# Second feed-forward matrix by seven products of quarters instead of eight

## The chip, the cores and the metric

The kernel runs on one core of one Trainium2 chip, as one program. The metric is the device time of one execution in microseconds (us); less is better. A core has five engines that run side by side, each through its own list of instructions in order, and that wait for one another by semaphores: TensorE (PE) for matrix products into PSUM, VectorE (DVE), ScalarE (ACT), GpSimd (POOL), and SyncE (SP), which here only issues transfers. PSUM has eight banks of 128 x 512 float32 numbers.

## What is computed

A network of two layers, for 1024 frames of a new stream and 8 x 16 frames of running ones (1152 frames of width 1024 together). Each layer is a mixer (attention and two kinds of recurrent memory) and a feed-forward part; the change lies in the feed-forward part alone:

```python
h = _rmsnorm(x, norm_ffn[layer])
x = x + jnp.square(jax.nn.relu(h @ w_ff1[layer])) @ w_ff2[layer]
```

`h` is 1152 x 1024, `w_ff1` 1024 x 4096, `w_ff2` 4096 x 1024.

## The kernel before

**Numbers in two parts.** Every large product runs on fp32r operands, which are the float32 numbers cut shorter. ACT copies a number into its fp32r high part, and a subtraction (`tensor_tensor` with `ALU.subtract`) makes the low part, the number less its high part. A product is then three matmuls, high x high, high x low and low x high (`PASSES`), added up in PSUM. Weights arrive by a transfer of 1 MB, a slab of 128 x 2048, in one of the two buffers of `raw`; ACT makes the high part (`hi_of`, L240), POOL the low part (`lo_of`, L245), both into one of the two buffers of `split`. The semaphores of this chain: `raw_in` (landed), `hi_ready`, `lo_ready`, `slab_begun` (PE has begun a slab, so the one before is free).

**Blocks.** The 4096 hidden features of a layer go in 8 blocks of 512 (`BLOCKS`), of which the first seven are a loop on each engine and the last is written out. A block takes four slabs: two of `w_ff1` (256 features each) and two of `w_ff2` (512 features x 512 outputs each).

- Hidden part (`proj_fm`, L452): for each of four groups of 128 features, 72 matmuls with 384 columns, 8 chunks of the width x 3 passes x 3 thirds of the frames, in three banks of PSUM (3, 4, 5 or 0, 1, 2 in turn). ACT takes the group out of PSUM with the relu (L624) into a row of 1152, DVE squares it (L651), ACT makes its high part (L614) and DVE its low part (L653). A low part reads two tensors in SBUF, as the square does.
- Second part (`pieces`, L571): 18 outputs of 128 frames x 512 features (9 tiles of frames, 2 halves), each 4 chunks x 3 passes = 12 matmuls of 512 columns: 216 in a block. DVE adds each finished bank to the stream `x` in SBUF (L658); this addition reads one tensor in SBUF and one in PSUM.

There are 16 such blocks in the program. The order of each engine is the order in which the code issues, and PE waits for `ff_lo` (low parts of the hidden rows), `lo_ready` (weights) and `ff_add` (a bank has been read). SP's loop `mlp` waits for `lo_ready` before it loads a slab in a buffer of `raw`.

## Time and profile before

| | |
|---|---|
| median of 3 runs | 3137.39 us (3136.26 to 3139.37) |
| the profiled execution, its own time | 3130.79 us |
| its span in the profile, mean granted clock | 3128.7 us, 0.978 |
| PE busy | 2967.5 us, 95% |
| matmuls of the hidden part and of projections like it (L452) | 7344, of which 288 in each block |
| matmuls of the second matrix (L571) | 3456 = 16 x 216 |

The profile is of one execution. Each engine's busy time is the time in which it ran instructions; a matmul's own duration overlaps that of the next, so its cost is read from the distance between starts, not from its mean. "PEclk" is the clock that TensorE was granted, 1.00 for 2.4 GHz and 0.50 for 1.2 GHz. The feed-forward parts lie at about 857 to 1657 us and 2330 to 3120 us of the span.

### The profile page before, as it was taken

To read this page: it belongs to the slowest core of one execution; us is meant where nothing else is said; L and a number is where in the kernel's file an instruction comes from. 1 tells how busy PE (TensorE), PEld (TensorE's weight loads), DVE (VectorE), ACT (ScalarE), POOL (GpSimd) and SP (SyncE) were. 2 spreads that over 40 slices of the span, in tenths; PEclk is the share of its full clock that TensorE was granted. 3 is DMA by queue.
4 is the path that set the end of the run, shared out by engine and by line. 5 is a ranking of instruction groups with operands and counts; after the bars stand their busy time and mean duration, and the time that the engine had idled before them with its cause. 6 is when DMAs were issued, how large, how long until landed. Compare 5 with 4: busy or idle time off the path is not lost.

```text
span 3128.7 us, 41812 instructions
## 1 busy us (share of the span) xinstructions
PE 2967.5 (95%) x17906; PEld 2751.8 (88%) x17906; DVE 1002.5 (32%) x1659; ACT 821.1 (26%) x1252; POOL 751.7 (24%) x476
## 2 busy tenths in 40 slices
PE   5999988888999999999999999897899999999998
PEld 5999977688999988999888999886898999899987
DVE  4500236564322222222232410295342222222223
ACT  4421346352312111121123302352231121111112
POOL 1122345132112111112112132473211112111111
PEclk8999999999999999999999999999999999999999
DMA  3112230233111111111103121203311111101111
GB/s 129 41 41 72 84 109 2 72 109 137 34 41 40 54 40 40 40 40 40 54 28 109 58 87 56 105 1 101 131 38 41 40 40 40 54 27 54 40 41 61
DMA packets 120320, 185.38 MB, mean 59 GB/s; under 512 B 11333, under 2 KB 84257, under 8 KB 119428
## 3 DMA queue, kind: packets, MB, share of 16 engines
q1 hardware_dynamic: 108784, 139.97, 13.6%
q0 software_dynamic: 11280, 43.50, 3.9%
q8 instruction: 94, 1.54, 0.2%
q14 instruction: 30, 0.25, 0.0%
q10 hardware_dynamic: 132, 0.13, 0.0%
HBM read 150.34 MB, written 33.20 MB: 59 GB/s over the span
## 4 chain that ended last, share of the span: by engine, by line
PE 87%; DVE 5%; ACT 2%; issue 2%; POOL 1%; DMA 1%; DVEq 0%; POOLq 0%; ACTq 0%; SPq 0%
PE ps L452 41%; PE ps L571 25%; PE ps L462 13%; PE ps L1383 1%; PE ps L1364 1%; DVE small L2259 1%; PE ps L401 1%; DMA units<-x_prompt 1%; PE ps L1689 1%; DVE units_r L527 0%; DVE spare L354 0%; PE ps L1729 0%; ACT spare L2128 0%; DVE spare L2520 0%; DMA units<-state_gla_s 0%
## 5 line engine op out<-in xcount | busy, mean ns | idle before, releaser
L452 PE MATMUL ps<-units_r,split 128*128 128x384 f32 x7344 | 1290.3, 336 | 10.8 <-DVEq L265 10.8
L452 PEld LDWEIGHTS ps<-units_r,split 128*128 128x128 f32 x7344 | 1283.6, 189 | 18.2 <-issue 18.1
L245 POOL TENSOR_TENSOR split<-raw,split 128x2048 fp32r<-128x2048 f32 x100 | 461.7, 4617 | 1728.2 <-ACT split L240 1728.2
L571 PE MATMUL ps<-split,units_r 128*128 128x512 f32 x3456 | 788.8, 389 | 0.4 <-DVE units L658 0.4
L571 PEld LDWEIGHTS ps<-split,units_r 128*128 128x128 f32 x3456 | 647.9, 188 | 134.8 <-issue 1.2
L462 PE MATMUL ps<-split,units_r 128*128 128x256 f32 x3456 | 425.1, 285 | 20.9 <-DVE units_r L527 19.3
L462 PEld LDWEIGHTS ps<-split,units_r 128*128 128x128 f32 x3456 | 420.0, 193 | 22.4 <-issue 19.4
L240 ACT ACTIVATE split<-raw 128x2048 fp32r<-128x2048 f32 x100 | 190.8, 1908 | 851.9 <-PE ps L571 433.6
L658 DVE TENSOR_TENSOR units<-units,ps 128x512 f32<-128x512 f32 x288 | 197.4, 687 | 496.7 <-PE ps L571 496.7
L651 DVE TENSOR_TENSOR spare<-spare 128x1152 f32<-128x1152 f32 x32 | 43.5, 1359 | 353.1 <-ACT spare L624 353.1
L651 DVE TENSOR_TENSOR glrow<-glrow 128x1152 f32<-128x1152 f32 x32 | 43.5, 1359 | 272.9 <-ACT glrow L624 272.9
L624 ACT ACTIVATE spare<-ps 128x1152 f32<-128x1152 f32 x32 | 36.2, 1132 | 281.4 <-PE ps L452 281.4
L624 ACT ACTIVATE glrow<-ps 128x1152 f32<-128x1152 f32 x32 | 36.2, 1132 | 280.2 <-PE ps L452 280.2
L521 DVE TENSOR_TENSOR units<-units,ps 128x256 f32<-128x256 f32 x72 | 30.3, 421 | 139.5 <-PE ps L462 135.8
L1670 PE MATMUL ps<-lend 128*128 128x128 f32 x480 | 61.0, 288 | 12.0 <-DVE lend L2509 8.9
L1670 PEld LDWEIGHTS ps<-lend 128*128 128x128 f32 x480 | 60.4, 205 | 13.4 <-issue 11.5
L1364 PE MATMUL ps<-masks,units 128*128 128x128 f32 x288 | 43.7, 279 | 19.1 <-DVE units L2269 11.3
L1896 ACT ACTIVATE units<-ps,small 128x128 f32<-128x128 f32 (+3 forms) x64 | 47.3, 739 | 42.8 <-DVE small L2259 42.7
L653 DVE TENSOR_TENSOR units_r<-glrow,units_r 128x1152 fp32r<-128x1152 f32 x32 | 43.5, 1358 | 39.5 <-ACT units_r L614 39.5
L653 DVE TENSOR_TENSOR units_r<-spare,units_r 128x1152 fp32r<-128x1152 f32 x32 | 43.5, 1358 | 39.5 <-ACT units_r L614 39.5
L2259 DVE TENSOR_REDUCE small<-ps 128x1 f32<-128x128 f32 (+3 forms) x64 | 48.4, 757 | 23.1 <-PE ps L1353 22.0
L324 ACT ACTIVATE glrow<-units 128x1024 f32<-128x1024 f32 x36 | 38.4, 1065 | 66.0 <-DVE units L658 44.1
(369 smaller groups left out, 2264.6 us busy)
## 6 DMA issues: line engine op xcount, KB each, us to landing
raw<-w_ff SPq DMA_DIRECT2D x64, 1024.0 KB, 5.4
raw<-w_in_even SPq DMA_DIRECT2D x14, 1024.0 KB, 5.2
raw<-w_in_odd SPq DMA_DIRECT2D x12, 1024.0 KB, 5.5
raw<-w_out SPq DMA_DIRECT2D x8, 1024.0 KB, 8.9
units<-x_prompt SPq DMA_DIRECT2D x4, 1536.0 KB, 9.2
stream<-units POOLq DMA_DIRECT2D x1, 4608.0 KB, 14.1
...
```

Source lines behind the costliest of these rows:

```text
L240: act.activation(split[:, n % 2, 0, :], raw[:, n % 2, :], ACT.Copy).then_inc(hi_ready, 1)
L245: pool.tensor_tensor(split[:, n % 2, 1, :], raw[:, n % 2, :], split[:, n % 2, 0, :], ALU.subtract).then_inc(lo_ready, 1)
L452: last = pe.matmul(ps[:, bank + n, 0:GN], weights(slab, a, k, c0, P), h[b][:, k, n * GN:(n + 1) * GN], start=(k == 0 and q == 0), stop=(k ...
L462: last = pe.matmul(out, h[b][:, k, n * P:(n + 1) * P], weights(slab, a, k, 0, COLS), start=(k == 0 and q == 0), stop=(k == KC - 1 and q == 2))
L571: one = pe.matmul(ps[:, bank, :], hid[b][:, k, n * P:(n + 1) * P], weights(base + 2 + half, a, k, 0, 512, 512), start=(k == 0 and q == 0), ...
L624: act.activation(as_groups(HTMP_[j % 2]), ps[:, b:b + 3, 0:GN], ACT.Relu).then_inc(ff_relu, 1)
L651: dve.tensor_tensor(tmp, tmp, tmp, ALU.mult).then_inc(ff_sq, 1)
L653: dve.tensor_tensor(hid[1][:, j], tmp, hid[0][:, j], ALU.subtract).then_inc(ff_lo, 1)
L658: dve.tensor_tensor(xx, xx, ps[:, bank, :], ALU.add).then_inc(ff_add, 1)
L1364: last = pe.transpose(ps[:, 4 + t // 4, (t % 4) * P:(t % 4 + 1) * P], PR[j % 4][:, t * P:(t + 1) * P], ident)
L1670: last = pe.matmul(out[:, h], EL[n % 2][:, l, h], EL[n % 2][:, l, h], start=True, stop=True)
L2259: dve.tensor_reduce(stat[:, 4 + j % 4:5 + j % 4], src, AX.X, ALU.min).then_inc(f_mx, 1)
```

## The change

In each of the seven looped blocks of a layer (14 blocks), the second part no longer multiplies the block of hidden values (1024 prompt frames x 512 features) by the block of weights (512 x 1024) in eight products of quarters. With the hidden values in quarters p11, p12 (frames 0 to 511, features 0 to 255 and 256 to 511), p21, p22 (frames 512 to 1023), and the weights in b11, b12, b21, b22, it makes seven products of sums and differences of quarters. The sums are made in place: of the hidden quarters by DVE (three instructions: p11 - p21, p21 + p22, and that less p11, and later a fourth, p12 less the result), of the weights' quarters by POOL (`minus`, four instructions). Each is then split in high and low part, by ACT and DVE on the left, by ACT and POOL on the right. The ninth tile (the 128 frames of the running streams) is computed from the plain quarters. Two running sums stay in PSUM: a product is added to a bank that already holds an earlier one, after that one has been read by an addition of DVE. The eighth block of each layer is as before.

The numbers of instructions in a looped block:

| | before | after |
|---|---|---|
| PE, matmuls of 512 columns | 216 | 192 |
| PE, matmuls of 384 columns | 288 | 288 |
| DVE, two tensors in SBUF | 8 of 1152 | 4 of 1152, 11 of 1024, 2 of 256 |
| DVE, additions out of PSUM | 18 | 31 |
| ACT | 4 relus, 4 high parts of 1152, 4 of 2048 | 4 relus, 7 + 8 high parts of 1024, 2 of 256, 2 of 2048 |
| POOL | 4 of 2048 | 2 of 2048, 12 of 1024 |

DVE's eleven instructions on quarters are four sums and seven low parts. The core of the diff; `slabs_done` counts the semaphores, which step 10 and 14 times a block now, and waits elsewhere in the kernel use it:

```diff
+        STEPS, SPLITS, READS = 10, 14, 31
+        BEGUN, HI, LO = STEPS - 4, STEPS - 4, SPLITS - 4
+        def slabs_done(n, more):
+            return n + 1 + (BLOCKS - 1) * more * sum(n >= base + 4 * (BLOCKS - 1) for base in (MLP0, MLP1))
...
+        X_BANK, Y_BANK = (6, 7, 0, 1), (2, 3, 4, 5)
+        SUMS_FIRST, SUMS_LAST = (0, 1, 2, 3), (2, 3, 0, 1)
...
+            return hidden_[:, 2 * c:2 * c + 2, 512 * r:512 * r + 512]
+        def right_slot(base, s, part):
+            return split[:, (base + s // 2) % 2, part, 1024 * (s % 2):1024 * (s % 2) + 1024]
...
                     if j >= 2:
                         pe.wait_ge(ff_relu, blk * HC + (layer * FF // P + j - 1))
-                    proj_fm(pe, hidden_bank(j), slab, (j % 2) * P, h).then_inc(ff_h, 1)
+                    proj_fm(pe, hidden_bank(j), base + j // 2, (j % 2) * P, h).then_inc(ff_h, 1)
+            def product(bank, left, slot, start, stop, first, more=False):
+                for k in range(2):
+                    for q, (a, b) in enumerate(PASSES):
+                        last = pe.matmul(ps[:, bank, :], left(b, k), right_slot(base, slot, a)[:, 512 * k:512 * k + 512],
+                                         start=(start and k == 0 and q == 0), stop=(stop and k == 1 and q == 2),
...
+            def summed_block(blk):
+                hidden_rows(blk, blk * SPLITS + splits)
+                def right(count):
+                    pe.wait_ge(lo_ready, blk * SPLITS + (splits + count))
+                def left(count):
+                    pe.wait_ge(ff_lo, blk * 9 + (lows + count))
+                def taken(count):
+                    pe.wait_ge(ff_add, blk * READS + (reads + count))
+                right(2)
+                left(1)
+                for n in SUMS_FIRST:
+                    if n == 2:
+                        pe.wait_ge(ff_relu, blk * HC + (layer * FF // P + HC))
+                    product(X_BANK[n], tile(a0, n), 0, True, True, n == 0).then_inc(ff_y, 1)
+                left(2)
+                product(5, ninth(0), 0, True, False, False)
+                right(4)
+                product(4, ninth(0), 1, True, True, True).then_inc(ff_y, 1)
+                right(7)
+                left(5)
+                product(5, ninth(1), 2, False, True, True).then_inc(ff_y, 1)
+                for n in SUMS_FIRST:
+                    if n >= 2:
+                        taken(3 + n)
+                    product(Y_BANK[n], tile(a1, n), 2, True, True, False).then_inc(ff_y, 1)
+                right(9)
+                for n in SUMS_FIRST:
+                    taken(7 + n)
+                    product(Y_BANK[n], tile(a2, n), 3, True, True, n == 0).then_inc(ff_y, 1)
+                right(10)
+                left(6)
+                for n in SUMS_FIRST:
+                    taken(1 + n)
+                    product(X_BANK[n], tile(a0, n), 0, False, True, n == 0, True).then_inc(ff_y, 1)
+                right(11)
+                left(7)
+                for n in SUMS_FIRST:
+                    taken(15 + n)
+                    product(X_BANK[n], tile(a1, n), 1, False, True, n == 0, True).then_inc(ff_y, 1)
+                right(12)
+                left(8)
+                for n in SUMS_FIRST:
+                    taken(11 + n)
+                    product(Y_BANK[n], tile(a2, n), 2, False, True, n == 0, True).then_inc(ff_y, 1)
+                right(13)
+                left(9)
+                taken(23)
+                product(2, ninth(1), 3, True, True, True).then_inc(ff_y, 1)
+                for n in SUMS_LAST:
+                    taken(19 + n)
+                    product(X_BANK[n], tile(a0, n), 3, False, True, False, True).then_inc(ff_y, 1)
+                taken(29)
...
+            def summed_block(blk):
+                def loaded(slab):
+                    act.wait_ge(raw_in[slab % 2], blk * 32 + raw_count(slab))
+                def freed(count):
+                    act.wait_ge(slab_begun, blk * STEPS + (begun + count))
+                def made(count):
+                    act.wait_ge(lo_ready, blk * SPLITS + (splits + count))
+                def squared(count):
+                    act.wait_ge(ff_sq, blk * 8 + (squares + count))
+                def relu(j):
+                    act.wait_ge(ff_h, blk * HC + (layer * FF // P + j + 1))
+                    b = hidden_bank(j)
+                    act.activation(as_groups(plain[:, j]), ps[:, b:b + 3, 0:GN], ACT.Relu).then_inc(ff_relu, 1)
+                def right_high(slot, src):
+                    act.activation(right_slot(base, slot, 0), src, ACT.Copy).then_inc(hi_ready, 1)
+                def left_high(slot, src):
+                    act.activation(slot, src, ACT.Copy).then_inc(ff_hi, 1)
+                loaded(base + 1)
+                freed(1)
+                act.activation(split[:, (base + 1) % 2, 0, :], raw[:, (base + 1) % 2, :], ACT.Copy).then_inc(hi_ready, 1)
+                relu(0)
+                relu(1)
+                loaded(base + 2)
+                freed(2)
+                right_high(0, right_raw(base, 0, 0))
+                squared(2)
+                left_high(a0[:, 0], quarter(plain, 0, 0))
+                left_high(left_ninth[:, 0, 0:2], plain[:, 0:2, SEQ:T])
+                loaded(base + 3)
+                right_high(1, right_raw(base, 0, 1))
+                squared(3)
+                left_high(a2[:, 0], left_third(layer))
+                relu(2)
+                relu(3)
+                freed(3)
+                right_high(2, right_raw(base, 1, 0))
+                squared(5)
+                left_high(a1[:, 0], quarter(plain, 0, 1))
+                left_high(left_ninth[:, 0, 2:4], plain[:, 2:4, SEQ:T])
+                made(5)
+                right_high(3, right_raw(base, 0, 1))
+                squared(7)
+                freed(4)
+                left_high(a0[:, 0], quarter(plain, 0, 0))
+                made(6)
+                right_high(0, right_sum)
+                freed(5)
+                right_high(1, right_raw(base, 0, 0))
+                freed(6)
+                left_high(a1[:, 0], quarter(plain, 1, 0))
+                made(8)
+                right_high(2, right_raw(base, 1, 0))
+                freed(7)
+                left_high(a2[:, 0], quarter(plain, 1, 1))
+                right_high(3, right_raw(base, 1, 1))
+                squared(8)
+                freed(8)
+                left_high(a0[:, 0], quarter(plain, 0, 1))
+                loaded(base + 4)
+                freed(9)
+                act.activation(split[:, base % 2, 0, :], raw[:, base % 2, :], ACT.Copy).then_inc(hi_ready, 1)
+                act.wait_ge(ff_lo, blk * 9 + (lows + 9))
...
+            def summed_block(blk):
+                def high(count):
+                    pool.wait_ge(hi_ready, blk * STEPS + (highs + count))
+                def made(count):
+                    pool.wait_ge(lo_ready, blk * SPLITS + (splits + count))
+                def slab_low(r):
+                    pool.tensor_tensor(split[:, r, 1, :], raw[:, r, :], split[:, r, 0, :], ALU.subtract).then_inc(lo_ready, 1)
+                def right_low(slot, src):
+                    pool.tensor_tensor(right_slot(base, slot, 1), src, right_slot(base, slot, 0), ALU.subtract).then_inc(lo_ready, 1)
+                def minus(out, x, y):
+                    pool.tensor_tensor(out, x, y, ALU.subtract).then_inc(lo_ready, 1)
+                b11, b12, b21, b22 = (right_raw(base, r, c) for r in range(2) for c in range(2))
+                high(1)
+                slab_low((base + 1) % 2)
+                high(2)
+                right_low(0, b11)
+                pool.wait_ge(raw_in[(base + 3) % 2], blk * 32 + raw_count(base + 3))
+                made(2)
+                minus(b11, b12, b11)
+                high(3)
+                right_low(1, b12)
+                made(4)
+                minus(b12, b22, b12)
+                minus(right_sum, b22, b11)
+                high(4)
+                right_low(2, b21)
+                made(7)
+                minus(b21, b21, right_sum)
+                high(5)
+                right_low(3, b12)
+                high(6)
+                right_low(0, right_sum)
+                high(7)
+                right_low(1, b11)
+                high(8)
+                right_low(2, b21)
+                high(9)
+                right_low(3, b22)
+                high(10)
+                slab_low(base % 2)
...
+            slabs = base + 4 * LASTB
+            pool.wait_ge(lo_ready, slabs_done(slabs, LO))
+            gain()
+            for j in range(1, 4 if layer else 5):
+                lo_of(pool, slabs + j)
...
+            def summed_block(blk):
+                def square(j):
+                    dve.wait_ge(ff_relu, blk * HC + (layer * FF // P + j + 1))
+                    dve.tensor_tensor(plain[:, j], plain[:, j], plain[:, j], ALU.mult).then_inc(ff_sq, 1)
+                def squared(count):
+                    dve.wait_ge(ff_sq, blk * 8 + (squares + count))
+                def low(count, slot, src, high):
+                    dve.wait_ge(ff_hi, blk * 9 + (highs + count))
+                    dve.tensor_tensor(slot, src, high, ALU.subtract).then_inc(ff_lo, 1)
+                def add(count, n, half, bank):
+                    dve.wait_ge(ff_y, blk * READS + (sums + count))
+                    xx = x[:, n, half * 512:(half + 1) * 512]
+                    dve.tensor_tensor(xx, xx, ps[:, bank, :], ALU.add).then_inc(ff_add, 1)
+                p11, p12, p21, p22 = (quarter(plain, r, c) for r in range(2) for c in range(2))
+                s3 = left_third(layer)
+                square(0)
+                square(1)
+                squared(2)
+                dve.tensor_tensor(s3, p11, p21, ALU.subtract).then_inc(ff_sq, 1)
+                low(1, a0[:, 1], p11, a0[:, 0])
+                low(2, left_ninth[:, 1, 0:2], plain[:, 0:2, SEQ:T], left_ninth[:, 0, 0:2])
+                low(3, a2[:, 1], s3, a2[:, 0])
+                square(2)
+                square(3)
+                low(4, a1[:, 1], p12, a1[:, 0])
+                low(5, left_ninth[:, 1, 2:4], plain[:, 2:4, SEQ:T], left_ninth[:, 0, 2:4])
+                dve.tensor_tensor(p21, p21, p22, ALU.add).then_inc(ff_sq, 1)
+                squared(6)
+                dve.tensor_tensor(p11, p21, p11, ALU.subtract).then_inc(ff_sq, 1)
+                for n in SUMS_FIRST:
+                    add(1 + n, n, 0, X_BANK[n])
+                add(5, PT, 1, 4)
+                add(6, PT, 0, 5)
+                dve.wait_ge(ff_add, blk * READS + (sums + 4))
+                for n in SUMS_FIRST:
+                    add(7 + n, n, 0, Y_BANK[n])
+                low(6, a0[:, 1], p11, a0[:, 0])
+                for n in SUMS_FIRST:
+                    add(11 + n, 4 + n, 1, Y_BANK[n])
+                dve.tensor_tensor(p12, p12, p11, ALU.subtract).then_inc(ff_sq, 1)
+                low(7, a1[:, 1], p21, a1[:, 0])
+                for n in SUMS_FIRST:
+                    add(15 + n, 4 + n, 0, X_BANK[n])
+                low(8, a2[:, 1], p22, a2[:, 0])
+                for n in SUMS_FIRST:
+                    add(19 + n, 4 + n, 1, X_BANK[n])
+                low(9, a0[:, 1], p12, a0[:, 0])
+                for n in SUMS_FIRST:
+                    add(23 + n, 4 + n, 0, Y_BANK[n])
+                add(27, PT, 1, 2)
+                for at, n in enumerate(SUMS_LAST):
+                    add(28 + at, n, 1, X_BANK[n])
...
                         n = base + j
-                        sp.wait_ge(lo_ready, blk * 4 + (n - 1))
+                        sp.wait_ge(lo_ready, blk * SPLITS + (slabs_done(base, LO) + j - 2))
```

**Order on DVE.** From the last two squares of a block to the first addition. Before, a hidden row is squared and split at once, and the additions follow:

```order
L651 TENSOR_TENSOR spare<-spare 128x1152 [waits ff_relu]
L653 TENSOR_TENSOR units6_r_52<-spare,units6_r_52 128x1152 [waits ff_hi]
L651 TENSOR_TENSOR glrow<-glrow 128x1152 [waits ff_relu]
L653 TENSOR_TENSOR units6_r_52<-glrow,units6_r_52 128x1152 [waits ff_hi]
L658 TENSOR_TENSOR units2<-units2,ps 128x512 [waits ff_y]
```

Now (units6 are the hidden values, units6_r_52 and glrow_r_55 their parts, units2 is `x`):

```order
L905 TENSOR_TENSOR units6<-units6 128x1152 [waits ff_relu]
L912 TENSOR_TENSOR units6_r_52<-units6,units6_r_52 128x1024 [waits ff_hi]
L912 TENSOR_TENSOR glrow_r_55<-units6,glrow_r_55 128x256 [waits ff_hi]
L932 TENSOR_TENSOR units6<-units6 128x2x512
L934 TENSOR_TENSOR units6<-units6 128x2x512 [waits ff_sq]
L917 TENSOR_TENSOR units2<-units2,ps 128x512 [waits ff_y]
```

Four instructions on two tensors in SBUF now stand between the last square and the first of ten additions.

**Order on POOL.** The rows in the loop of one block. Before, four of one kind:

```order
L971 DMA sel<-norm_mix 128x1024 [waits dve_stage,pool_stage,act_stage,pe_stage]
L552 UNCONDITIONAL_BRANCH
L552 ISA
L245 TENSOR_TENSOR split_53<-raw,split_53 128x2048 [waits hi_ready]
L244 REGISTER_ALU
```

Now, from the seventh to the tenth of fourteen, which POOL comes to when the last hidden row is done (sel holds the sum `right_sum`; the load of a norm's gains into sel stands behind the loop now):

```order
L854 TENSOR_TENSOR split_53<-raw,split_53 128x1024 [waits hi_ready]
L848 REGISTER_ALU
L857 TENSOR_TENSOR raw<-raw,sel 128x1024 [waits lo_ready]
L845 REGISTER_ALU
L854 TENSOR_TENSOR split_53<-raw,split_53 128x1024 [waits hi_ready]
L845 REGISTER_ALU
L854 TENSOR_TENSOR split_53<-sel,split_53 128x1024 [waits hi_ready]
```

Each of these too reads two tensors in SBUF; before, one of L245 stood in this stretch.

**Order on PE.** Behind the first seven products, at the second running sum. Before, a bank takes 12 matmuls and the wait for its reader comes from the ninth output on:

```order
L571 MATMUL ps<-split,units_r 128x512 [waits ff_lo]
L571 MATMUL ps<-split,units_r 128x512 x44
L592 REGISTER_ALU
L571 MATMUL ps<-split,units_r 128x512 [waits ff_lo]
L571 MATMUL ps<-split,units_r 128x512 x38
L588 ISA
L571 MATMUL ps<-split,units_r 128x512 [waits ff_add]
L571 MATMUL ps<-split,units_r 128x512 x11
```

Now a product is 6 matmuls, and from the tenth product on each waits for an addition:

```order
L616 MATMUL ps<-split,glrow_r 128x512 [waits ff_lo]
L616 MATMUL ps<-split,glrow_r 128x512 x5
L616 MATMUL ps<-split,units_r 128x512 x12
L616 MATMUL ps<-split,units_r 128x512 [waits ff_add]
L616 MATMUL ps<-split,units_r 128x512 x5
```

The first row with `ff_add` is the tenth product; it writes bank 4, and waits for the block's fifth addition.

## Rows read from the trace of the kernel before

**Rows 1.** The page: share of the span by engine, and what PE's clock was.

```profile
PE 2967.5 (95%) x17906; PEld 2751.8 (88%) x17906; DVE 1002.5 (32%) x1659; ACT 821.1 (26%) x1252; POOL 751.7 (24%) x476
...
PEclk8999999999999999999999999999999999999999
```

**Rows 2.** The page's groups: line, engine, shapes, count | busy us, mean ns | idle before.

```profile
L571 PE MATMUL ps<-split,units_r 128*128 128x512 f32 x3456 | 788.8, 389 | 0.4 <-DVE units L658 0.4
...
L240 ACT ACTIVATE split<-raw 128x2048 fp32r<-128x2048 f32 x100 | 190.8, 1908 | 851.9 <-PE ps L571 433.6
L658 DVE TENSOR_TENSOR units<-units,ps 128x512 f32<-128x512 f32 x288 | 197.4, 687 | 496.7 <-PE ps L571 496.7
...
L324 ACT ACTIVATE glrow<-units 128x1024 f32<-128x1024 f32 x36 | 38.4, 1065 | 66.0 <-DVE units L658 44.1
```

**Rows 3.** The trace in order, second part of one block: start us, us, engine, instruction.

```profile
1302.64 49.16 PE L571 MATMUL ps<-split,units_r 128*128 128x512 f32 x216
1302.84 1.13 ACT L624 ACTIVATE glrow<-ps 128x1152 f32<-128x1152 f32 x1 [8.75 <-PE ps L452]
1304.00 1.36 DVE L651 TENSOR_TENSOR glrow<-glrow 128x1152 f32<-128x1152 f32 x1 [8.53 <-ACT glrow L624]
...
1316.48 0.69 DVE L658 TENSOR_TENSOR units<-units,ps 128x512 f32<-128x512 f32 x1 [2.03 <-PE ps L571]
1319.20 0.69 DVE L658 TENSOR_TENSOR units<-units,ps 128x512 f32<-128x512 f32 x1 [2.03 <-PE ps L571]
...
1349.12 3.41 DVE L658 TENSOR_TENSOR units<-units,ps 128x512 f32<-128x512 f32 x5 [2.03 <-PE ps L571]
...
1351.72 50.21 PE L452 MATMUL ps<-units_r,split 128*128 128x384 f32 x288
```

**Rows 4.** Groups with shapes apart: DVE and POOL instructions of other widths, same columns.

```profile
L391 DVE TENSOR_TENSOR units_r<-ps,units_r 128x1024 fp32r<-128x1024 f32 x27 | 32.7, 1218 | 6.1 <-ACT units_r L385 5.9
...
L2508 DVE TENSOR_TENSOR lend<-ps,units 128x256 f32<-128x256 f32 x60 | 25.1, 419 | 8.8 <-ACT ps L2109 7.3
...
L1038 POOL TENSOR_TENSOR split<-units,split 64x1024 fp32r<-64x1024 f32 x7 | 16.5, 2358 | 0.6
```

**Rows 5.** One line each, ns min/median/max: POOL's L245 and DVE's L527.

```profile
L245 POOL TENSOR_TENSOR split<-raw,split x100: 4512/4608/4952, 27.6 to 3076.6; 128x2048 fp32r<-128x2048 f32 x100
...
L527 DVE TENSOR_TENSOR units_r<-units,units_r x36: 670/685/5002, 729.3 to 2226.8; 128x512 fp32r<-128x512 f32 x36
```

**Rows 6.** The trace in order where DVE and POOL meet, three places.

```profile
36.19 4.51 POOL L245 TENSOR_TENSOR split<-raw,split 128x2048 fp32r<-128x2048 f32 x1 [4.10 <-ACT split L240]
...
36.94 4.84 DVE L354 SCALAR_TENSOR_TENSOR units<-units,small 128x1024 f32<-128x1024 f32 x1
...
132.33 1.28 DVE L2186 SCALAR_TENSOR_TENSOR units<-units,small 128x1024 f32<-128x1024 f32 x1
133.28 4.80 POOL L245 TENSOR_TENSOR split<-raw,split 128x2048 fp32r<-128x2048 f32 x1 [21.48 <-ACT split L240]
133.53 4.70 DVE L2188 SCALAR_TENSOR_TENSOR units<-units,small 128x128 f32<-128x128 f32 x1
...
2194.05 9.44 POOL L245 TENSOR_TENSOR split<-raw,split 128x2048 fp32r<-128x2048 f32 x2 [0.92 <-ACT split L240]
...
2195.14 9.51 DVE L527 TENSOR_TENSOR units_r<-units,units_r 128x512 fp32r<-128x512 f32 x3 [3.29 <-ACT units_r L484]
```

**Rows 7.** Stretches of PE: us from:to, length, busy us (x), granted clock, DMA share, GB/s.

```profile
2117.80:2127.80 10.00, 9.14 (x56) 1.00 0.00 0
2127.80:2131.70 3.90, 0.03 (x1) 1.00 0.00 0
2132.02:2135.42 3.40, 3.40 (x11) 0.50 0.01 2
2135.44:2138.83 3.39, 1.34 (x12) 1.00 0.00 0
2149.09:2152.48 3.39, 3.06 (x7) 0.50 0.62 173
444.30:447.30 3.00, 0.01 (x1) 1.00 1.03 380
447.30:457.00 9.70, 8.94 (x87) 1.00 0.04 14
```

163 lines of the change are left out of this document (101 added, 62 removed).

## The prediction

> **What bounds the kernel now.** I read the page's first parts, then the groups, then one block of the feed-forward part in order of time, then the places where VectorE (DVE) and GpSimd (POOL) run at once, and last the granted clock around gaps of TensorE (PE). PE is busy for 95% of the span and every other engine for a third or less [rows 1]. In the feed-forward part it is busier than that: one block's second part is 216 matmuls from 1302.64 to 1351.72, the hidden part follows at once [rows 3], and in all 3456 matmuls of the second matrix PE stood idle for 0.4 us [rows 2]. So a matmul removed there is worth its full price, as long as nobody makes PE wait. What a matmul costs is the distance between starts: an output of 12 matmuls is added every 2.72 us (1316.48, 1319.20) [rows 3], so 2.72 / 12 = 0.2267 us each. A block takes 49.1 us for the second part and 50.2 us for the hidden part.
>
> **What is removed.** 216 - 192 = 24 matmuls in each of 14 blocks: 24 x 0.2267 = 5.44 us a block, 76.2 us in all. The 288 hidden matmuls and the two last blocks stay. That is all that the change takes away.
>
> **What is added.** DVE gets 9 more instructions on two tensors in SBUF and 13 more additions a block. By length: four squares of 1.36 us, 11 instructions of 1024 at 1.22, 2 of 256 at 0.42 [rows 3, 4] and 31 additions at 0.68 (five in 3.41 us) [rows 3] make 5.4 + 13.4 + 0.8 + 21.1 = 41 us out of some 94. (That a 1024-wide instruction on two SBUF tensors takes what one out of PSUM takes is an estimate; L354, of another kind, takes 1.28.) ACT grows to about 25 us, POOL to 2 x 4.61 + 12 x 2.36 = 37.5 us, its 2.36 taken from L1038 with 1024 elements [rows 4, 5]. No engine is near full. The transfers keep their number and size. They start behind other counts of `lo_ready`, but each gets 10 us or more before its weights are wanted, so I price them at nothing; if that cover is gone, PE waits in the hidden part. The load of the gains on POOL's queue moves behind the loop, with a hidden part of 50 us ahead of its first reader: nothing. What is left is whether a chain of small steps makes PE wait, and there is one place where it does: the tenth product.
>
> **The chain to the tenth product, step by step.** Take as zero the start of the first product, that is the end of the hidden part. PE does nine products of 6 x 0.2267 = 1.36 us and comes to the tenth at 12.24. That one needs the fifth addition, and ahead of the fifth addition DVE has, in its own order: last square, low part of 1024, low part of 256, two sums, five additions.
> - The last relu starts 0.20 after zero and takes 1.13 [rows 3]: 1.33. The square: 2.72.
> - If DVE never met POOL: high part by ACT at 3.8 (two copies of 1.065 [rows 2]), low part 5.05, short low part 5.5, sum 6.7, sum 7.9, additions at 0.68 each; the fifth would end at about 11.3. PE, at 12.24, wouldn't wait: 0.9 us of slack.
> - But they meet. In the trace of before, a DVE instruction that reads two tensors in SBUF and starts while POOL works doesn't end before POOL has ended. L354 takes 4.84 instead of 1.28 us and ends at 41.78, 1.08 behind POOL's end at 40.70; L2188 takes 4.70 for 128 elements. It goes the other way too: POOL takes 4.80 where DVE had begun before it [rows 6]. L527 is 685 ns in the middle and 5002 at most [rows 5]. Where both have several in a row they take turns: two POOL instructions from 2194.05 took 9.44, which is 4.52 and 4.61 and 0.31 for the one of DVE that came between; three of DVE took 9.51 [rows 5, 6]. An addition out of PSUM isn't held (the middle of L658 stays 0.69 while L245 runs) [rows 2].
> - A turn is not quite as long as the sum: what waits is partly begun. The rows give 0.13 to 0.20 off for DVE behind POOL, 0.14 off for POOL behind DVE (133.61 to 138.08 is 4.47, not 4.61), 0.24 where it goes to and fro [rows 6].
> - So, in turns: POOL's low part of the third quarter 2.72 + 2.36 - 0.14 = 4.94. DVE's low part + 1.22 - 0.13 = 6.03. POOL's difference + 2.36 - 0.24 = 8.15. DVE's short low part + 0.42 - 0.13 = 8.44. POOL's next low part + 2.12 = 10.56. DVE's sum + 1.09 = 11.65. Its second sum, for which POOL has nothing to put in between (its next high part waits for this sum), + 1.26 = 12.91. Five additions + 3.41 = 16.32, and PE starts at about 16.4.
>
> PE waits 16.4 - 12.24 = 4.1 us in each block, where before it waited for nothing. (A part of it, 0.3 us, falls already at the seventh product, which needs the short low part of 8.44 and is reached at 8.16.) Later waits are covered: by the same walk each later product's low parts and additions are ready 2 us or more before PE comes to them, and the last slab's low part 5 us before the next hidden part.
>
> **The clock.** A gap of 3.9 us in dense work was followed by 3.4 us at a granted clock of 0.50, 1.2 instead of 2.4 GHz; such a stretch recurs at 2149.09. A gap of 3.0 us was not followed by one [rows 7]. My gap of 3.8 is like the first. At half clock the matmuls of 3.4 us lose 1.7 us; of the stretch at 2149.09, 0.33 us of 3.39 had no matmul in it, so the price can be less. Bounds: 0 and 1.7 us a block; I take 1.3, since the gap is far nearer to 3.9 than to 3.0 and part of the slow stretch may lie in the gap.
>
> **The sum.** - 5.44 + 4.1 + 1.3 = - 0.04 us a block, 14 blocks: - 0.6 us. The profiled execution of 3130.79 us would be 3130.2. The median of the runs shown is 6.6 us above it, so I forecast 3137.39 - 0.6 = 3136.8 us: the matmuls saved are given back in a wait and a slower clock.
>
> **A rule weighed.** The Trainium skill, page SBUF — State Buffer, section Who interferes with whom, says that a VectorE instruction with two SBUF inputs contends with a GpSimd instruction that reads SBUF, and that whoever is first has the pair of ports for its whole instruction while "the other fully blocks". The rows agree in kind (4.84 us instead of 1.28), and this rule speaks against the change, which puts 17 such instructions of the one beside 14 of the other. Taken by the letter, nothing is saved at a turn, which is rival C's time; the rows show 0.13 to 0.24 saved.
>
> **The rivals.**
> - A: the clock stays at full speed after a gap of this length, as after the 3.0 us [rows 7]. Against it, the 3.9. Per block - 5.44 + 4.1 = - 1.34, in all - 18.8: 3118.6 us.
> - B: DVE and POOL don't hinder each other in these instructions; then PE never waits and the whole 76.2 us stay: 3061.2 us. [Rows 6] speak strongly against it.
> - C, slower: turns are taken at full length. The chain is then 2.72 + 2.36 + 1.22 + 2.36 + 0.42 + 2.36 + 1.22 + 1.26 + 3.41 = 17.33, the wait 5.1, with the clock 6.4: + 1.0 a block, + 14 us, 3151 us. It decides as soon as wait and clock are over 5.44 together, and my 5.4 is just under that. The same comes if POOL's 1024-wide instruction takes 2.6 us instead of 2.36 (three are in the chain, 0.7 us a block), or if PE starts again late.
> - D: DVE gets two turns in a row once (its sum directly behind the short low part, with POOL's instruction behind both). The wait is 2.1 shorter, 2.0 us, and the clock stays, as after 3.0 us: - 3.44 a block, 3089 us. Against it: POOL has its instruction queued 2 us earlier, and in the pair at 2194.05 it came between [rows 6].
>
> That the change doesn't do what it says is no rival: the order of PE shows 192 in the loop for 216.
>
> **Chances.** Forecast 0.36, A 0.24, C 0.28, D 0.07, B 0.05. What a measurement of this kernel can tell from no change is about 0.2%, 6.3 us, or 0.45 us a block. So faster (A, B, D) 0.36, same 0.36, slower (C) 0.28. The range: A's 3118.6 with some 5 us for a turn that is shorter than I take it, and C's 3151 with a bit more for a second gap or a longer slow stretch: 3112 to 3156. B and D are left out.
>
> **What would show it.** In the profile of the changed kernel: the second part of a block as 192 matmuls over about 49 us rather than 43.5; in the waits, PE on the product's line waiting for DVE's addition, 14 times some 3.8 us; DVE's instructions of 1024 at 1.2 us where alone and 3 us where POOL runs; POOL's of 1024 at 2.4 to 3.2; slow stretches of the clock once a block, so that the mean granted clock falls from 0.978 to about 0.97. Wrong would be: no wait at the tenth product (then B), a wait without slow stretches (A), waits at other products or in the hidden part (then I missed a chain), or matmuls at a distance other than 0.227 us.

## The result, and the profile after

The changed kernel takes 3147.87 us (median of 7 runs, 3144.63 to 3149.89), the kernel before on the same chips 3137.66 us (7 runs, 3136.09 to 3139.62). The ratio is 1.0032, 95% interval 1.002 to 1.0043: slower by some 10 us, with 336 matmuls fewer.

The page of the changed kernel; the first line answers to [rows 1], the others to [rows 2] and give line, engine, shapes, count | busy us, mean ns | idle before:

```profile
PE 2931.5 (93%) x17570; PEld 2706.7 (86%) x17570; DVE 1453.2 (46%) x1967; ACT 924.2 (29%) x1406; POOL 1091.1 (35%) x616
...
L616 PE MATMUL ps<-split,units_r 128*128 128x512 f32 x1344 | 338.2, 412 | 44.6 <-DVE units L917 44.6
...
L616 PE MATMUL ps<-split,spare_r 128*128 128x512 f32 x1008 | 241.9, 395 | 0.0
```

PE is busy for 36 us less, but its share has fallen from 95 to 93%: the span has grown. The second matrix had 0.4 us of idle PE before; now 44.6 us stand ahead of its matmuls, waiting for DVE's additions (L917). Its matmuls come in two lengths, 389 ns in the middle (412 is a mean with those at half clock in it) and 395.

One block's second part in order of time (PE, ACT, DVE, POOL), to be held against [rows 3]; the first product starts at 1011.30:

```profile
1011.30 5.76 PE L616 MATMUL ps<-split,spare_r 128*128 128x512 f32 x24
...
1012.67 1.36 DVE L905 TENSOR_TENSOR units<-units 128x1152 f32<-128x1152 f32 x1 [7.55 <-ACT units L753]
1013.66 2.64 POOL L854 TENSOR_TENSOR split<-raw,split 128x1024 fp32r<-128x1024 f32 x1 [9.76 <-ACT split L756]
...
1015.15 2.23 DVE L912 TENSOR_TENSOR units_r<-units,units_r 128x1024 fp32r<-128x1024 f32 x1 [1.13 <-ACT units_r L759]
...
1016.38 3.25 POOL L857 TENSOR_TENSOR raw<-raw,sel 128x1024 f32<-128x1024 f32 x1
1016.90 4.73 PE L616 MATMUL ps<-split,glrow_r 128*128 128x512 f32 x18
1017.30 2.61 DVE L912 TENSOR_TENSOR glrow_r<-units,glrow_r 128x256 fp32r<-128x256 f32 x1
1019.59 2.58 POOL L854 TENSOR_TENSOR split<-raw,split 128x1024 fp32r<-128x1024 f32 x1
1019.84 3.42 DVE L932 TENSOR_TENSOR units<-units 128x1024 f32<-128x1024 f32 x1
1021.47 2.88 PE L616 MATMUL ps<-split,units_r 128*128 128x512 f32 x12
1023.28 1.23 DVE L934 TENSOR_TENSOR units<-units 128x1024 f32<-128x1024 f32 x1
1024.43 4.86 DVE L917 TENSOR_TENSOR units<-units,ps 128x512 f32<-128x512 f32 x8
...
1027.55 4.61 PE L616 MATMUL ps<-split,units_r 128*128 128x512 f32 x12 [3.20 <-DVE units L917]
```

DVE's short low part (256 elements, 0.42 us of work) takes 2.61 us, its sum of 1024 3.42; they end 0.28 and 1.09 us behind the end of an instruction of POOL (at 1019.63 and 1022.17). The second sum, with POOL idle, takes 1.23. The tenth product starts at 1027.55, 16.25 behind the first, after an idle of 3.20.

The clock over that block and over the fifth block of the layer; columns as in [rows 7], the first four rows with all engines' busy time between:

```profile
1011.32:1024.30 12.98, 12.88 (x55) 9.86 (x54) 10.47 (x5) 4.40 (x5) 8.43 (x3) 1.00 0.00 0
1024.40:1027.50 3.10, 0.00 (x0) 0.00 (x0) 3.10 (x7) 2.88 (x3) 0.80 (x1) 1.00 0.00 0
1028.25:1031.60 3.35, 3.35 (x10) 2.60 (x9) 1.73 (x3) 0.00 (x0) 3.16 (x2) 0.50 0.00 0
1031.70:1060.90 29.20, 29.20 (x128) 23.87 (x128) 19.66 (x26) 7.01 (x6) 9.93 (x3) 1.00 0.36 108
...
1325.25:1331.95 6.70, 5.91 (x14) 0.50 0.00 0
```

Just after the gap the granted clock is 0.50 for 3.4 us, in 12 of the 14 blocks, and for 6.8 us in the fifth block of each layer. In the fourth of each layer it begins while PE still waits, and costs less. Before the change no such stretch lay in these blocks (granted clock 1.00 from 950 to 1500 us; now 0.98).

**Where the time went, per block.** From the start of the first product to the start of the next hidden part a block takes 49.63 us (1011.30 to 1060.93), 50.81 in the fifth of each layer and 49.4 in the fourth; the mean of the 14 is 49.77, of before 49.05. That is + 0.72 us, 14 x 0.72 = 10 us, which is the difference of the medians. The hidden part is as it was. The two profiled executions differ by more, 3147.87 - 3130.79 = 17 us. The rest lies outside these blocks: 5.4 us ahead of the first one (it starts at 911.72 and at 906.35), and 1.6 us in a slow stretch of the clock behind the last block of the first layer. Both come and go from trace to trace (starts from 908.07 in E2 to 914.25 in E3; the stretch is in the traces of E3, E6 and E7 and not in those of E1, E2, E4, E5, E8, E9 and E10). So differences of a few us are read from the blocks, and not from the times.

### The profile page after: what moved, and what is told of

Same layout as the page of the kernel before. It is cut to its first block, busy times and chain, and to the rows that moved or that the text cites. A ratio compares the mean times of both kernels' runs of the same rounds, so it can differ in the third digit from the quotient of the medians.

```text
span 3146.1 us, 42736 instructions
## 1 busy us (share of the span) xinstructions
PE 2931.5 (93%) x17570; PEld 2706.7 (86%) x17570; DVE 1453.2 (46%) x1967; ACT 924.2 (29%) x1406; POOL 1091.1 (35%) x616
## 4 chain that ended last, share of the span: by engine, by line
PE 82%; DVE 8%; issue 4%; ACT 3%; POOL 1%; DMA 1%; DVEq 0%; POOLq 0%; ACTq 0%; SPq 0%
PE ps L463 41%; PE ps L616 17%; PE ps L473 13%; PE ps L695 3%; DVE units L917 1%; DVE glrow_r L912 1%; PE ps L1697 1%; DVE small L2573 1%; PE ps L1678 1%; PE ps L412 1%; DMA units<-x_prompt 1%; DVE units L905 1%; PE ps L2003 1%; ACT units L753 1%; ACT units_r L759 0%
## 5 line engine op out<-in xcount | busy, mean ns | idle before, releaser
L473 PEld LDWEIGHTS ps<-split,units_r 128*128 128x128 f32 x3456 | 422.1, 194 | 26.5 <-issue 19.4
L854 POOL TENSOR_TENSOR split<-raw,split 128x1024 fp32r<-128x1024 f32 x98 | 264.7, 2701 | 514.6 <-ACT split L756 514.6
L256 POOL TENSOR_TENSOR split<-raw,split 128x2048 fp32r<-128x2048 f32 x44 | 203.5, 4626 | 605.9 <-ACT split L251 605.9
L616 PE MATMUL ps<-split,units_r 128*128 128x512 f32 x1344 | 338.2, 412 | 44.6 <-DVE units L917 44.6
L616 PEld LDWEIGHTS ps<-split,units_r 128*128 128x128 f32 x1344 | 268.7, 201 | 109.7 <-DVE units L917 50.5
L917 DVE TENSOR_TENSOR units<-units,ps 128x512 f32<-128x512 f32 x434 | 287.7, 684 | 163.0 <-PE ps L616 162.3
L905 DVE TENSOR_TENSOR units<-units 128x1152 f32<-128x1152 f32 x56 | 106.7, 1906 | 451.0 <-ACT units L753 451.0
L616 PE MATMUL ps<-split,spare_r 128*128 128x512 f32 x1008 | 241.9, 395 | 0.0
L616 PEld LDWEIGHTS ps<-split,spare_r 128*128 128x128 f32 x1008 | 189.1, 188 | 44.4
L851 POOL TENSOR_TENSOR split<-raw,split 128x2048 fp32r<-128x2048 f32 x28 | 129.1, 4610 | 280.6 <-ACT split L763 168.1
L251 ACT ACTIVATE split<-raw 128x2048 fp32r<-128x2048 f32 x44 | 83.9, 1906 | 284.2 <-PE ps L473 214.3
L912 DVE TENSOR_TENSOR units_r<-units,units_r 128x1024 fp32r<-128x1024 f32 x56 | 113.0, 2018 | 15.8 <-ACT units_r L759 15.8
L756 ACT ACTIVATE split<-raw 128x1024 fp32r<-128x1024 f32 x98 | 102.6, 1047 | 0.0
L695 PE MATMUL ps<-split,units_r 128*128 128x512 f32 x432 | 102.1, 396 | 0.4 <-DVE units L972 0.4
L695 PEld LDWEIGHTS ps<-split,units_r 128*128 128x128 f32 x432 | 81.6, 190 | 18.0 <-issue 1.2
L759 ACT ACTIVATE spare_r<-units 128x1024 fp32r<-128x1024 f32 x42 | 44.6, 1063 | 172.2 <-DVE units L934 115.3
```

Source lines behind the costliest of these rows:

```text
L256: pool.tensor_tensor(split[:, n % 2, 1, :], raw[:, n % 2, :], split[:, n % 2, 0, :], ALU.subtract).then_inc(lo_ready, 1)
L473: last = pe.matmul(out, h[b][:, k, n * P:(n + 1) * P], weights(slab, a, k, 0, COLS), start=(k == 0 and q == 0), stop=(k == KC - 1 and q == 2))
L616: last = pe.matmul(ps[:, bank, :], left(b, k), right_slot(base, slot, a)[:, 512 * k:512 * k + 512], start=(start and k == 0 and q == 0), s ...
L695: one = pe.matmul(ps[:, bank, :], hid[b][:, k, n * P:(n + 1) * P], weights(base + 2 + half, a, k, 0, 512, 512), start=(k == 0 and q == 0), ...
L756: act.activation(right_slot(base, slot, 0), src, ACT.Copy).then_inc(hi_ready, 1)
L759: act.activation(slot, src, ACT.Copy).then_inc(ff_hi, 1)
```

## The experiments

Each time is a median; "before" was run on the same chip beside it. The names E1 to E10 are only for this text.

**E1: move two tensors by 32 bytes.** The matmuls with the left tile in `spare_r` or `glrow_r` lie 0.232 to 0.2335 us apart in the changed kernel (24 from 1011.30 to 1016.90 is 0.2333), the others 0.227. Of the operands of the second matrix's products only these two start at 32 bytes past a multiple of 64. (The expectation below says so of all operands of TensorE; `small` and `junk256_r`, which it reads elsewhere, start so too.)

```diff
         masks = sb("masks", [P, C_N])
+        sb("gap", [P, 8])
         sel = sb("sel", [P, 8, P])
```

> The changed kernel with an unused tensor of 8 floats ahead of sel, spare and glrow, so that the left quarters in spare_r and glrow_r start 32 bytes later: 208576 instead of 208544 bytes, a multiple of 64 like all other operands of TensorE; nothing else. In the changed kernel the matmuls whose left side is in these two lie 0.232 to 0.2335 us apart, the others 0.227. Theory (the start of the left tile costs the 6 ns): all 192 go to 0.227, 96 x 0.0062 = 0.6 us a block less, 8 to 9 us in all: 3139 us. Rival (it is the place in PSUM or the accumulation of these products): the distance stays 0.233 and the time stays 3148 us. The wait at the tenth product stays 3.2 us either way.

Measured: 3149.2 us, ratio to before 1.0043 (1.003 to 1.0055), and the distance is still 0.233. The theory of the start address modulo 64 falls, at least for tensors that lie this high. E5, E6 and E10 took the address up again.

The trace of E1 shows something else. In its first block the gap ahead of the tenth product is as long as in the others, and no slow stretch follows it; a line of PE's timeline and one of its windows:

```profile
929.00 8.45 PE L617 MATMUL ps<-split,units_r 128*128 128x512 f32 x36 [3.18 <-DVE units L918]
```

```profile
929.10:935.00 5.90, 5.90 (x26) 1.00 0.02 4
```

That block takes 48.07 us, ten others 49.4 to 49.7 and three 50.8 to 51.0. So a gap of 3.2 us is followed by the slow clock in 27 of the 28 blocks of these two traces, once it is not, and its length varies.

**E2: fill the gap with useless work.** The ninth product is made three times.

```diff
+                    if n == 1:
+                        product(Y_BANK[n], tile(a1, n), 2, True, True, False)
+                        product(Y_BANK[n], tile(a1, n), 2, True, True, False)
                     product(Y_BANK[n], tile(a1, n), 2, True, True, False).then_inc(ff_y, 1)
```

> The changed kernel with the ninth product of each looped block made three times into the same bank (the result is the same), the bank given free after the third: 12 more matmuls, 2.72 us of work put in the gap before the tenth product. Nobody needs that bank before the fifth addition is done, so the tenth product should start at the same 16.2 us after the first. Theory (clock): the gap is too short for a slow stretch, the clock of 0.50 goes away in the 14 blocks and 1.5 us a block come back: 3148 - 21 = 3127 us, with MORE matmuls. Rival (the slow stretches cost nothing, the loss is all in the waits): 3148 us, or more if the third product delays others.

Measured: 3123.2 us, ratio to before 0.9961 (0.9947 to 0.9974), where the changed kernel stands at 1.0032. 168 more matmuls made it some 25 us faster. The trace of E2, in order of time on PE, and a stretch of 550 us in the windows (length, busy, clock):

```profile
1006.09 5.76 PE L616 MATMUL ps<-split,spare_r 128*128 128x512 f32 x24
1011.69 4.73 PE L616 MATMUL ps<-split,glrow_r 128*128 128x512 f32 x18
1016.25 5.60 PE L616 MATMUL ps<-split,units_r 128*128 128x512 f32 x24
1022.34 8.47 PE L616 MATMUL ps<-split,units_r 128*128 128x512 f32 x36 [0.49 <-DVE units L920]
...
1054.13 50.11 PE L463 MATMUL ps<-units_r,split 128*128 128x384 f32 x288
```

```profile
950.00:1500.00 550.00, 547.04 (x2794) 1.00 0.13 42
```

The tenth product starts 16.25 behind the first (1022.34 - 1006.09), as in the changed kernel: the wait for the addition is the same. But the gap is 0.49, there is no slow stretch in any of the 14 blocks, and the block's second part takes 48.04 in place of 49.77. So the slow clock costs 49.77 - 48.04 = 1.73 us a block, 24 us in all; the medians say 25, the two ratios to before 22. The one block of E1 without a slow stretch, 48.07, says the same.

**E3: another order on VectorE.** The five additions for which the tenth product waits stand ahead of the sums; the second sum stands behind two more additions, and the fourth sum behind the low part of the eighth quarter.

```diff
-                dve.tensor_tensor(p21, p21, p22, ALU.add).then_inc(ff_sq, 1)
-                squared(6)
-                dve.tensor_tensor(p11, p21, p11, ALU.subtract).then_inc(ff_sq, 1)
                 for n in SUMS_FIRST:
                     add(1 + n, n, 0, X_BANK[n])
                 add(5, PT, 1, 4)
+                dve.tensor_tensor(p21, p21, p22, ALU.add).then_inc(ff_sq, 1)
                 add(6, PT, 0, 5)
                 dve.wait_ge(ff_add, blk * READS + (sums + 4))
-                for n in SUMS_FIRST:
+                add(7, 0, 0, Y_BANK[0])
+                squared(6)
+                dve.tensor_tensor(p11, p21, p11, ALU.subtract).then_inc(ff_sq, 1)
+                for n in SUMS_FIRST[1:]:
                     add(7 + n, n, 0, Y_BANK[n])
...
-                dve.tensor_tensor(p12, p12, p11, ALU.subtract).then_inc(ff_sq, 1)
                 low(7, a1[:, 1], p21, a1[:, 0])
...
                 low(8, a2[:, 1], p22, a2[:, 0])
+                dve.tensor_tensor(p12, p12, p11, ALU.subtract).then_inc(ff_sq, 1)
```

> The changed kernel with VectorE's order changed alone: the first five additions of a block ahead of the sum p21 + p22, the second sum behind two more additions, the fourth sum (p12) behind the low part of the eighth quarter. Theory (the wait is the chain through five turns ahead of the fifth addition, and no engine is too full): the fifth addition ends near 12, TensorE waits 0.3 us at the seventh product and 0.5 us or less at later ones, no slow stretch; of 5.5 us a block 4.7 or more come back: 3148 - 14 x 4.7 = 3082 us. Rival (VectorE and GpSimd together are too full, the wait only moves to a later product): one wait of 2 to 4 us a block elsewhere with its slow stretch, 3130 to 3148 us.

Measured: 3076.3 us, ratio to before 0.9809 (0.9795 to 0.9823). The same instructions, in another order, are 1.9% faster than before where the changed kernel is 0.3% slower. The trace of E3, in order of time:

```profile
1008.75 5.76 PE L616 MATMUL ps<-split,spare_r 128*128 128x512 f32 x24
...
1014.34 4.74 PE L616 MATMUL ps<-split,glrow_r 128*128 128x512 f32 x18
1014.75 2.61 DVE L912 TENSOR_TENSOR glrow_r<-units,glrow_r 128x256 fp32r<-128x256 f32 x1
1017.03 2.57 POOL L854 TENSOR_TENSOR split<-raw,split 128x1024 fp32r<-128x1024 f32 x1
1017.28 3.06 DVE L917 TENSOR_TENSOR units<-units,ps 128x512 f32<-128x512 f32 x5
1018.92 11.06 PE L616 MATMUL ps<-split,units_r 128*128 128x512 f32 x48
1020.27 1.21 DVE L935 TENSOR_TENSOR units<-units 128x1024 f32<-128x1024 f32 x1
```

The additions, which read one tensor in SBUF and one in PSUM, run while POOL works (five in 3.06 us, 0.61 each as without POOL); and the sum that comes after them finds POOL done, and takes 1.21 us for 3.42. PE goes through the tenth product without a pause. A block's second part takes 44.55 us.

**E4: take POOL out of the chain.** Three of its instructions are done over 8 of 1024 columns; that part of the second matrix is left out of the result.

```diff
-                right_low(2, b21)
+                pool.tensor_tensor(right_slot(base, 2, 1)[:, 0:8], b21[:, 0:8], right_slot(base, 2, 0)[:, 0:8], ALU.subtract).then_inc(lo_ready, 1)
                 made(7)
-                minus(b21, b21, right_sum)
+                minus(b21[:, 0:8], b21[:, 0:8], right_sum[:, 0:8])
                 high(5)
-                right_low(3, b12)
+                pool.tensor_tensor(right_slot(base, 3, 1)[:, 0:8], b12[:, 0:8], right_slot(base, 3, 0)[:, 0:8], ALU.subtract).then_inc(lo_ready, 1)
```

> The changed kernel with three of GpSimd's instructions in the chain (low part of b21, b21 less the sum, low part of b12) done over the first 8 of 1024 columns only: part of the second matrix is left out. All instructions, waits and their order on every engine stay. Theory (VectorE is held while GpSimd's instruction runs): VectorE's 1024-wide instructions in the chain drop from 2.2 to 3.4 us to 1.22, the 256-wide from 2.6 to 0.4, the tenth product isn't waited for, and no slow stretch: 3148 - 14 x (4.0 + 1.5) = 3071 us. Rival (VectorE's own queue is too long, its instructions are slow for another reason): they stay long, 3148 us.

Measured: 3067.7 us, ratio 0.9783 (0.9766 to 0.98). The trace of E4, on DVE, same four instructions as in the block above:

```profile
1009.53 1.23 DVE L912 TENSOR_TENSOR units_r<-units,units_r 128x1024 fp32r<-128x1024 f32 x1 [1.12 <-ACT units_r L759]
1010.67 0.42 DVE L912 TENSOR_TENSOR glrow_r<-units,glrow_r 128x256 fp32r<-128x256 f32 x1
...
1011.01 1.23 DVE L932 TENSOR_TENSOR units<-units 128x1024 f32<-128x1024 f32 x1
...
1012.27 1.22 DVE L934 TENSOR_TENSOR units<-units 128x1024 f32<-128x1024 f32 x1
```

DVE's code is untouched, and its instructions fall from 2.23, 2.61 and 3.42 to 1.23, 0.42 and 1.23. No wait at any product, no slow stretch. The long instructions of DVE were POOL's doing.

**E5, E6, E10: where the left tile lies.** All three start from E3. E5 allocates `spare` and `glrow` ahead of `raw`, so that they start at 151680 and 159872 bytes instead of 208544 and 216736. E10 moves `spare` alone, to 168064. E6 exchanges the contents of two left slots, so that a1 (8 products) and not a0 (12) lies in `spare_r`. The edits, of E5 and of E6:

```diff
+        at_spare = -(-nc.sbuf_base // 32) * 32
+        spare = sb("spare", [P, 2048])
...
         raw = sb("raw", [P, 2, SLAB])
```

```diff
-            rows = (spare_r[:, :], span(at, at + 2048, pairs_r), span(at + 2048, at + 4096, pairs_r))
+            rows = (span(at, at + 2048, pairs_r), spare_r[:, :], span(at + 2048, at + 4096, pairs_r))
```

> The reordered kernel of the earlier run (3076.3 us) with spare and glrow allocated ahead of raw, so that they start at 151680 bytes and not at 208544, and raw, split, masks and sel 12.8 KB further up; nothing else. Theory (the 6 ns come from the address range that the left tile is read from): with spare_r in a lower range all matmuls of the second matrix lie 0.227 us apart, 96 x 0.0062 = 0.6 us a block less, 8.5 us in all: 3068 us. Rival (it is what is computed with them, the order or the bank): 0.233 stays, 3076 us.

> The reordered kernel with the first and the second left slot exchanged: a0 (12 products a block) in the units, a1 (8 products) in spare_r. Theory (place): now the 8 products of a1 and the 4 of the ninth tile lie 0.233 us apart, 72 in place of 96 matmuls, 24 x 0.0062 x 14 = 2 us less: 3074 us. Rival (role): the products of a0 stay at 0.233 wherever they lie, 3076 us; the distances tell, not the time.

> The reordered kernel with spare alone allocated ahead of split (at 168064 bytes; split, masks and sel 8 KB further up), glrow where it was (216736). Theory (it is the address of the left tile): matmuls with the left side in spare_r 0.227 us apart, those in glrow_r still 0.233; 72 x 0.0062 x 14 = 6 us less than 3076: 3070 us. Rival (it is something that both have since they are one allocation group, or where split lies): both change or neither.

Measured: E5 3068.6 us, ratio 0.9784 (0.9766 to 0.9801); E6 3074.8, 0.9799 (0.978 to 0.9817); E10 3070.0, 0.9786 (0.977 to 0.9802). These intervals overlap one another and that of E3, so it is the traces that tell. One line of the matmuls each, ns min/median/max and count. E3:

```profile
L616 PE MATMUL ps<-split,units_r x1344: 389/389/397, 924.4 to 2959.0; 128*128 128x512 f32 x192
...
L616 PE MATMUL ps<-split,spare_r x1008: 392/395/397, 914.3 to 2966.0; 128*128 128x512 f32 x168
```

E6:

```profile
L616 PE MATMUL ps<-split,spare_r x672: 392/395/397, 923.5 to 2954.0; 128*128 128x512 f32 x168
```

E10:

```profile
L616 PE MATMUL ps<-split,spare_r x1008: 387/389/398, 909.0 to 2955.2; 128*128 128x512 f32 x168
...
L616 PE MATMUL ps<-split,glrow_r x336: 392/395/502, 914.5 to 2949.8; 128*128 128x512 f32 x168
```

E5:

```profile
L616 PE MATMUL ps<-split,spare_r x1008: 387/389/398, 908.3 to 2954.0; 128*128 128x512 f32 x168
...
L616 PE MATMUL ps<-split,glrow_r x336: 387/389/504, 913.7 to 2948.6; 128*128 128x512 f32 x168
```

The 6 ns follow the place, not the role: whatever lies in `spare_r` at 208544 is slow (E6), `spare_r` at 168064 is fast while `glrow_r` at 216736 stays slow (E10), and with both low all 192 matmuls are fast (E5). In E5 the right side, `split`, reaches up to 213632 bytes and costs nothing. So it is the left tile's address; between which addresses it changes (176256 is below, 208544 above) and why, no run tells.

What it costs is less than 96 x 0.0062 = 0.6 us a block, on which the expectations rest. A block's second part takes 44.55 in E3, 44.18 in E5, 44.24 in E10 and 44.56 in E6. In all four the seventh product starts some 8.7 us behind the first, when VectorE's short low part is done, so 0.233 in place of 0.227 ahead of it only fills a wait. Behind that point lie 60 matmuls of the 0.233 kind in E3 and in E6, 12 in E10 and none in E5: 60 x 0.0062 = 0.37 and 48 x 0.0062 = 0.30, as measured. E6, from which I expected 2 us, moved only matmuls that cost nothing. And E5's 3068, as expected, is in part luck: 14 x 0.37 = 5 us come from the address, the rest of the 8 lies outside the blocks, 1.6 of it in the slow stretch that E3 has behind a layer's last block and E5 has not.

**E7: the last small wait.** E5, and the first product of the second running sum ahead of the ninth tile's third product.

```diff
                 right(7)
+                left(4)
+                product(Y_BANK[0], tile(a1, 0), 2, True, True, False).then_inc(ff_y, 1)
                 left(5)
                 product(5, ninth(1), 2, False, True, True).then_inc(ff_y, 1)
```

> The placement of e5_place, and TensorE makes the first product of the second running sum ahead of the third of the ninth tile, which waits for the short low part. Expected by the walk of the first prediction: that part ends at 8.4 after the first product, TensorE now comes to it at 9.5, so the last wait of 0.3 to 0.5 us a block goes, 14 x 0.4 = 5 to 6 us less than e5_place: about 3063 us, or 3071 if the placement brought nothing. If the wait moves elsewhere: as e5_place.

Measured: 3067.4 us, ratio 0.978 (0.9763 to 0.9796); from E5 it can't be told apart, and the 5 to 6 us that I expected aren't there. The block's second part is 44.05 for 44.18: the wait at the seventh product is gone, and one at a later addition has come:

```profile
1017.00 2.88 PE L616 MATMUL ps<-split,units_r 128*128 128x512 f32 x12
...
1020.08 2.14 PE L616 MATMUL ps<-split,units_r 128*128 128x512 f32 x8 [0.20 <-DVE units L919]
```

**E8: take away one turn.** The changed kernel, with POOL's b21 less the sum over 8 columns; that part of the result is left out.

```diff
-                minus(b21, b21, right_sum)
+                minus(b21[:, 0:8], b21[:, 0:8], right_sum[:, 0:8])
```

> The changed kernel (not the reordered one) with one of GpSimd's instructions in the chain, b21 less the sum, done over 8 of 1024 columns: part of the second matrix is left out. Theory (turns): one turn of 2.1 us is gone from the chain, the tenth product starts at about 14.1 instead of 16.2 after the first; the gap falls from 3.2 to about 1.2 us and no slow stretch follows: 14 x (2.1 + 1.5) = 50 us less, 3098 us. Rival (turns don't add up, the chain is bound elsewhere): less than 1 us a block from the wait; rival on the clock: the slow stretches stay and only 14 x 2.1 = 29 us go, 3119 us.

Measured: 3091.0 us, ratio 0.9857 (0.9837 to 0.9876). In the trace of E8:

```profile
1010.05 0.42 DVE L912 TENSOR_TENSOR glrow_r<-units,glrow_r 128x256 fp32r<-128x256 f32 x1
1010.39 3.42 DVE L932 TENSOR_TENSOR units<-units 128x1024 f32<-128x1024 f32 x1
...
1018.11 8.47 PE L616 MATMUL ps<-split,units_r 128*128 128x512 f32 x36 [1.36 <-DVE units L917]
```

The short low part is free, the sum still pays its turn. The tenth product starts 14.06 behind the first, not 16.25: 2.19 us for one turn, where the walk gives 2.1. The gap is 1.36, and no slow stretch follows it in the 14 blocks.

**E9: half of the reordering.** E3 with the fourth sum (p12) back in its old place.

```diff
+                dve.tensor_tensor(p12, p12, p11, ALU.subtract).then_inc(ff_sq, 1)
                 low(7, a1[:, 1], p21, a1[:, 0])
```

> The reordered kernel without its last edit: the first five additions stand ahead of the sum p21 + p22 and the second sum behind two more, but the fourth sum (p12) stands where the changed kernel had it, ahead of the low part that the seventeenth to twentieth of the 28 prompt products (running sum of the first banks) need. Theory (VectorE has little slack in the stretch behind its meeting with GpSimd): its additions 15 to 18 come 1.2 us later and TensorE waits for the fifteenth, up to 2 us a block and perhaps with a slow stretch: 3076 + 14 x 2 = 3104 us, up to 3125 with the clock. Rival (the first edit alone brings all): 3076 us.

Measured: 3091.5 us, ratio 0.9856 (0.9839 to 0.9872). In its trace the wait is at the product that follows the fifteenth addition; the low part ahead of that addition takes 3.42 us:

```profile
1025.97 1.86 DVE L946 TENSOR_TENSOR units<-units 128x1024 f32<-128x1024 f32 x1
1027.75 3.42 DVE L912 TENSOR_TENSOR units_r<-units,units_r 128x1024 fp32r<-128x1024 f32 x1
1031.09 2.47 DVE L917 TENSOR_TENSOR units<-units,ps 128x512 f32<-128x512 f32 x4
1031.82 4.39 PE L616 MATMUL ps<-split,units_r 128*128 128x512 f32 x18 [0.90 <-DVE units L917]
```

A block is 45.72 - 44.55 = 1.2 us longer than in E3, without a slow stretch, 15 us in all as measured; I had written 2 us. So the order ahead of the tenth product brought most (3147.9 to 3091.5, as the two ratios to before have it), and moving one sum brought another 15 us. The sum delays the low part by more than its own 1.2 us, since both now meet POOL: it takes 1.86, and the low part 3.42 where it takes 1.83 in E3. That low part ends 27.06 behind the first product in E9 and 23.70 in E3.

## Why the prediction was wrong, point by point

The time lay in the range, and the mechanism was there: the saving eaten by a wait at the tenth product and the clock behind it. But the forecast was no change, with faster as likely, and the kernel is slower beyond its interval. By its own steps:

- **Removed: 5.44 us a block.** Right. 192 matmuls at 0.227 would be 43.5, and E5 has 44.18, of which 0.5 is the wait at the seventh product (it starts at 8.69 and not at 8.16).
- **The chain.** Right, nearly to the row. Behind the first product: square 2.73 (forecast 2.72), POOL's low part 5.00 (4.94), low part 6.08 (6.03), difference 8.33 (8.15), short low part 8.61 (8.44), next low part 10.87 (10.56), sum 11.96 (11.65), second sum 13.21 (12.91), tenth product 16.25 (16.4). The additions made up for the rest: with all banks waiting DVE does eight in 4.86 us, 0.61 each and not 0.68. That the turns are the cause is shown by E4 and, for the size of one, by E8.
- **The wait: forecast 4.1, is 3.7.** PE comes to the tenth product at 12.54 where it isn't held (E4), not at 12.24, since its first seven products are the slower kind. 16.25 - 12.54 = 3.7.
- **Matmuls at 0.227: one of the two steps that failed.** I took the distance between matmuls from before for all of them. Half, 96 of 192, have their left side in `spare_r` or `glrow_r` and lie 0.233 apart: 96 x 0.0062 = 0.6 us a block. The diff shows that `spare_r` and `glrow_r` are new places for left operands, and [rows 3] were of left operands in the units alone. Some 0.3 of it, the 42 matmuls ahead of the tenth product, falls into the wait, which is why that came out shorter: the tenth product starts when VectorE lets it. The other 54 cost 0.33 us a block. E5 shows the distance undone.
- **The clock: forecast 1.3, is 1.73; the other step that failed.** The bounds were 0 and 1.7. In ten blocks all of a slow stretch fell on work (49.63 - 48.04 = 1.6), in the fourth of each layer a part lay in the gap (1.35), and in the fifth of each it was twice as long (2.8). E2 shows the size without the wait in it. I had let a part of the stretch lie in the gap everywhere, and had no term for a double one.
- **The sum.** - 5.44 + 0.60 + 3.71 + 1.73 = + 0.60, against + 0.72 measured (0.1 is left over, as in E2: 48.04 where 44.19 + 3.71 is 47.90), against - 0.04 forecast. Of the 0.76 between, 0.6 is the matmuls' distance, 0.4 the clock, 0.1 the rest left over, and the wait gives 0.4 back. Counted by what each cost in the end, it is the clock 0.43, the distance 0.33 (54 matmuls), and the tenth product, 0.1 earlier than forecast, against the 0.1 left over. With either error alone the forecast would have been + 0.3 or + 0.4 a block, which is within the 0.45 that it called no change (an estimate; the changed kernel with its left tiles placed low was not run). It took both.
- **Rivals.** A (no slow clock) and B (no hindrance) are excluded by the trace; E2 and E4 show what each would have been, 3123 and 3068 us (I had 3118.6 and 3061). D (two turns in a row) didn't occur: the turns went one by one in the block shown, and in all 14 the tenth product starts 16.23 to 16.25 behind the first. C had the right sign and the time 3151, but its reason, turns at full length, is wrong: a turn costs what I took.
- **Chances.** A net of - 0.04 us a block between a saving of 5.44 and a loss of 5.4 meant that any forgotten term decided the sign. The prediction did name "matmuls at a distance other than 0.227 us" among the signs of being wrong, but it gave them no cost, no rival and no chance. The chance of slower, 0.28, was too low for that. That the time lay in the range says little: it is 44 us wide and holds faster, same and slower.
- **What else was named to look for.** 192 matmuls over about 49 us: 49.77. Waits of some 3.8: 3.2, and some 0.3 at the seventh. POOL's of 1024 at 2.4 to 3.2: 2.37 to 3.38. Mean clock about 0.97: 0.969. No other waits: right.
